# Reordering the queues of a ConvFFN up stage: additions out of PSUM ahead of the gated product, and a new order of operand sums and norm in the first pair

## The reference, cut to what matters

```python
D_FF = 2816
def conv_ffn(hn, buf, w_up, conv_w, conv_b, w_down):
    T = hn.shape[1]
    up = hn @ w_up                                   # 1024 -> 2 x 2816
    full = jnp.concatenate([buf.astype(up.dtype), up], axis=1)
    conv = sum(full[:, j:j + T] * conv_w[j] for j in range(CONV_W)) + conv_b
    a, gt = jnp.split(conv, 2, axis=-1)
    return (a * jax.nn.silu(gt)) @ w_down, full[:, T:]
...
    f, conv_state = conv_ffn(rmsnorm(x, P['norm_ffn'][l]), s_conv, ...)
    x = x + f
y = rmsnorm(x, P['norm_final'])
```

## Time and profile before

| | us |
|---|---|
| median of 3 runs (lowest, highest) | 2222.54 (2219.32, 2223.23) |
| the profiled execution, its own time | 2222.29 |
| its span, first to last instruction | 2220.2 |
| TensorE busy in the span | 2147.5 (97%) |
| VectorE, ScalarE, GpSimd busy | 1240.8, 757.2, 557.8 |

### The profile page before, as it was taken

The page is one execution under the profiler, slowest core; times in us unless marked ns, Lnnn a source line. Parts: engine busy times, 40 slices in busy tenths (PEclk is TensorE's granted clock), DMA queues, the critical chain, the costliest instruction groups (busy, mean ns, idle before and its releaser), DMA issues.

```text
span 2220.2 us, 35643 instructions
## 1 busy us (share of the span) xinstructions
PE 2147.5 (97%) x15110; PEld 2091.2 (94%) x15110; DVE 1240.8 (56%) x1526; ACT 757.2 (34%) x1094; POOL 557.8 (25%) x604
## 2 busy tenths in 40 slices
PE   7999999999999999999999999989999999999997
PEld 6999999999999999999999988989999999999997
DVE  6514755444456264246643234488888888854446
ACT  6313344233322322233321144254444444421113
POOL 6689910000000000000000000055555555410001
PEclk9999999999999999999999999999999999999999
DMA  7322114122422223244312152221222212343212
GB/s 277 115 77 66 66 57 172 60 77 89 153 98 77 69 87 115 77 162 174 123 47 86 48 225 116 87 69 63 81 71 71 79 64 81 111 174 124 86 66 77
DMA packets 66260, 222.79 MB, mean 100 GB/s; under 512 B 7584, under 2 KB 13024, under 8 KB 62416
## 3 DMA queue, kind: packets, MB, share of 16 engines
q1 hardware_dynamic: 46144, 129.70, 17.5%
q0 software_dynamic: 14816, 62.51, 7.5%
q10 hardware_dynamic: 5184, 28.98, 3.3%
HBM read 168.38 MB, written 51.78 MB: 99 GB/s over the span
## 4 chain that ended last, share of the span: by engine, by line
PE 77%; DVE 15%; issue 3%; ACT 2%; POOL 2%; DMA 1%; DVEq 0%; ACTq 0%; POOLq 0%
PE ps L305 19%; PE ps L308 19%; PE ps L306 19%; DVE WQ L3175 3%; PE ps L2785 2%; DVE CA L3224 2%; DVE CA L3223 2%; PE ps L2789 2%; PE ps L2786 2%; POOL UBA L2709 1%; PE ps L1981 1%; PE ps L2337 1%; PE ps L2313 1%; DVE UBA L3216 1%; DVE WL L299 1%
## 5 line engine op out<-in xcount | busy, mean ns | idle before, releaser
L305 PE MATMUL ps<-XH,WH 128*128 128x352 f32 (+1 forms) x1752 | 566.8, 325 | 5.6 <-ACT STAGE L365 3.1
L306 PE MATMUL ps<-XL,WH 128*128 128x352 f32 (+1 forms) x1560 | 491.9, 320 | 0.0
L308 PE MATMUL ps<-XH,WL 128*128 128x352 f32 (+1 forms) x1752 | 371.1, 320 | 0.0
L305 PEld LDWEIGHTS ps<-XH,WH 128*128 128x128 f32 x1752 | 330.2, 188 | 14.3 <-issue 10.2
L299 DVE TENSOR_TENSOR WL<-WRAW,WH 128x1024 fp32r<-128x1024 f32 x133 | 166.5, 1252 | 271.6 <-ACT WH L294 270.1
L306 PEld LDWEIGHTS ps<-XL,WH 128*128 128x128 f32 x1560 | 294.5, 189 | 0.1
L308 PEld LDWEIGHTS ps<-XH,WL 128*128 128x128 f32 x1752 | 292.4, 188 | 0.0
L294 ACT ACTIVATE WH<-WRAW 128x1024 fp32r<-128x1024 f32 x133 | 140.8, 1058 | 329.9 <-PE ps L308 311.7
L2785 PE MATMUL ps<-B,WQ 128*128 128x258 f32 x528 | 140.3, 287 | 19.3 <-DVE UBG L3216 18.9
L305 PE MATMUL ps<-HX,WH 128*128 128x352 f32 (+1 forms) x480 | 153.9, 322 | 3.0 <-DVE HX L3237 3.0
L306 PE MATMUL ps<-HX,WH 128*128 128x352 f32 (+1 forms) x480 | 151.9, 322 | 0.0
(11 more groups left out here) (622 smaller groups left out, 4868.6 us busy)
## 6 DMA issues: line engine op xcount, KB each, us to landing
WRAW<-in_wslabs SPq DMA_DIRECT2D x133, 512.0 KB, 3.6
WRAW<-in_wup SPq DMA_DIRECT2D x88, 256.0 KB, 2.7
scratch_spill<-STAGE SPq DMA_DIRECT2D x40, 516.0 KB, 2.7
ZS<-scratch_spill POOLq DMA_DIRECT2D x24, 516.0 KB, 5.3
scratch_h<-HOUT ACTq DMA_DIRECT2D x22, 516.0 KB, 2.7
HRAW<-scratch_h POOLq DMA_DIRECT2D x22, 516.0 KB, 5.8
XIN<-in_xT SPq DMA_DIRECT2D x8, 516.0 KB, 4.5
XR<-in_xT ACTq DMA_DIRECT2D x2, 2064.0 KB, 7.9
```

Source lines behind the costliest of these rows:

```text
L305: pe.matmul(out[t], WH[:, slot, w, :], xh(k, t), start=(k == 0), stop=False)
L306: pe.matmul(out[t], WH[:, slot, w, :], xl(k, t), start=False, stop=False)
L308: last = pe.matmul(out[t], WL[:, slot, w, :], xh(k, t), start=False, stop=(k == nk - 1))
```

## The change

Four things are done.

1. In VectorE's queue `product(f-1)` moves from ahead of d2 to behind b. In ScalarE's queue `store(f-1)`, which waits for it, moves behind the copies of P7 and the high parts of P7 and P2; the high part of P4 moves ahead of `now`.
2. Pair 0: the rests of B22 and of N3 2, 3 move from GpSimd to VectorE (table `E_PL` goes); the two last N4 differences move behind the norm; `norm_columns` stands ahead of P6 and the row of the norm is spread into banks 0 and 1 once b has read P2; P2 of pair 1, not P4 of pair 0, waits for the row. The weight operands of pair 1 are split in the order P1, P5, P6, P3, P7, P2, and GpSimd's sums of pair 1 no longer stand behind the scaling.
3. The loads of the convolution weights FW and FB move from GpSimd's queue to SyncE's.
4. Last pair: two of the four reloaded rows are raised and their rests made ahead of `product(20)` and `store(20)`, two behind.

```diff
 # sums: GpSimd
+        def pool_late_sums(pool, f):
+
             nc.gpsimd.tensor_tensor(A21, A21, A11, ALU.subtract).then_inc(s_sum.sem, 1)
...
-            for k in range(4):
-                rest("B22", k, y_of(k))
-            for k in range(2, 4):
-                rest("N3", k, XR[:, k, HALF:N])
+            pool_sums(pool, 1)
             pool.wait_ge(norm_rb, 2)
             pool_scale(pool, 0, 0)
-            pool.wait_ge(e_lo, E_LO["N4", 3])
-            pool.wait_ge(e_pl.sem, e_pl.at(6))
-            pool.dma_start(FW[:], I["ffn_w"]).then_inc(ffn_in.sem, 16)
-            pool.dma_start(FB[:], I["ffn_buf"]).then_inc(ffn_in.sem, 16)
-            pool_sums(pool, 1)
+            pool_late_sums(pool, 1)
...
 # TensorE, pair 0
+            norm_columns()
             pe.wait_ge(s_lo, W_AT["P6", 0])
             pe.wait_ge(u_ac, 1)
-            product("P6", slot_of("P6", 0), lambda k: pe.wait_ge(e_lo, E_LO["T2", k]))
-            norm_columns()
+            product("P6", slot_of("P6", 0), lambda k: pe.wait_ge(e_lo, E_AT["T2", k]))
...
+            pe.wait_ge(u_dv, DV_AT["b", 0])
             norm_spread()
...
 # ScalarE, pair f
             for f in range(1, NF):
-                if f == 1:
-                    act_product_hi(act, "P6", 1)
-                    act_product_hi(act, "P3", 1)
+                act_product_hi(act, "P4", f)
                 now(f - 1, 0)
                 if f > 1:
                     act.wait_ge(u_cv.sem, u_cv.at(2 * f - 2))
-                act_product_hi(act, "P4", f)
                 act_take(act, "P1", f, first_half(UB[f % 2][0]))
...
-                store(f - 1)
                 act_take(act, "P7", f, first_half(UB[f % 2][1]))
                 if f < NF - 1:
                     act_product_hi(act, "P7", f + 1)
                     act_product_hi(act, "P2", f + 1)
                 else:
+                    for kk in range(2):
+                        raise_h(0, kk)
                     slab_hi(1)
-            for kk in range(4):
+                store(f - 1)
+            for kk in range(2, 4):
                 raise_h(0, kk)
...
 # VectorE, pair f
-                product(f - 1)
-                if f == NF - 1:
-                    slab_lo(0)
                 join("d2", f)
                 if f < NF - 1:
                     dve_product_lo(dve, "P3", f + 1)
+                else:
+                    slab_lo(0)
                 join("a3", f)
                 if f < NF - 1:
                     dve_product_lo(dve, "P7", f + 1)
+                join("b", f)
+                if f == NF - 1:
+                    for kk in range(2):
+                        rest_h(0, kk)
+                product(f - 1)
+                if f < NF - 1:
+                    dve_product_lo(dve, "P2", f + 1)
                 else:
                     dve.wait_ge(u_pe, U_AT["P7", f])
                     slab_lo(1)
-                join("b", f)
-                if f < NF - 1:
-                    dve_product_lo(dve, "P2", f + 1)
                 join("c", f)
```

More of the change, by code:

```diff
@@ L2582, in program @@
         EARLY = [(x, m) for m in range(4) for x in ("B11", "T1")] + [("B21", k) for k in range(3)]
-        E_HI = {x: n + 1 for n, x in enumerate(
+        E_AT = {x: n + 1 for n, x in enumerate(
             EARLY + [("T2", 0), ("T2", 1), ("T2", 2), ("B21", 3), ("T2", 3)] +
             [(x, k) for x in ("B22", "N3", "N4") for k in range(4)])}
-        E_LO = {x: n + 1 for n, x in enumerate(
-            EARLY + [("B21", 3)] + [("T2", k) for k in range(4)] + [("N3", 0), ("N3", 1)] + [("N4", k) for k in range(4)])}
-        E_PL = {x: n + 1 for n, x in enumerate([("B22", k) for k in range(4)] + [("N3", 2), ("N3", 3)])}
+        C_AT = {x: n + 1 for n, x in enumerate(
+            [(x, k) for k in range(2) for x in ("N3", "T2", "N4")] +
+            [("N3", 2), ("T2", 2), ("N3", 3), ("T2", 3), ("N4", 2), ("N4", 3)])}
         u_pe, u_ac, u_dv = sem("u_pe"), sem("u_ac"), sem("u_dv")
@@ L2775, in pe_ffn, with product @@
         def pe_ffn(pe):
-            def product(p, w, k_wait=None, after=None):
+            def product(p, w, k_wait=None):
                 x = OPS[OP_OF[p]]
@@ L2802, in norm_spread @@
                 for c in range(2):
-                    last = pe.matmul(ps[:, 6 + c, :], ONES, SS[:, 512 * c:512 * c + 512], start=True, stop=True)
+                    last = pe.matmul(ps[:, c, :], ONES, SS[:, 512 * c:512 * c + 512], start=True, stop=True)
                 last.then_inc(norm_pe, 1)
@@ L2807, in norm_samples @@
                 pe.wait_ge(norm_act, 2 * 3 + 2)
[L2808 removed]
+                pe.matmul(ps[:, 0, 0:B], ONES, SS[:, T:N], start=True, stop=True).then_inc(norm_tail, 1)
             pe.wait_ge(s_lo, W_AT["P1", 0])
[L2811 removed]
+            pe.wait_ge(e_lo, E_AT["B11", 3])
             evacuated(pe, G_CO + 7)
@@ L3034, in act_ffn @@
             act_take(act, "P1", 0, first_half(UB[0][0]))
-            act.wait_ge(e_c.sem, e_c.at(3 * 3 + 2))
-            act_raise(act, "T2", 3, XR[:, 3, 0:HALF])
             act_product_hi(act, "P3", 0)
             act_product_hi(act, "P7", 0)
+            act.wait_ge(e_c.sem, e_c.at(C_AT["T2", 3]))
+            act_raise(act, "T2", 3, XR[:, 3, 0:HALF])
+            for k in range(4):
+                act.wait_ge(e_y.sem, e_y.at(k + 1))
+                act_raise(act, "B22", k, y_of(k))
             act.wait_ge(xr_out.sem, xr_out.at(16 * KT))
@@ L3041, in act_ffn @@
             act_take(act, "P5", 0, second_half(UB[0][1]))
-            for k in range(4):
-                act.wait_ge(e_y.sem, e_y.at(k + 1))
-                act_raise(act, "B22", k, y_of(k))
-            for k in range(4):
-                act.wait_ge(e_c.sem, e_c.at(3 * k + 1))
-                act_raise(act, "N3", k, XR[:, k, HALF:N])
-            act_product_hi(act, "P1", 1)
-            act_take(act, "P6", 0, second_half(UB[0][0]))
             act.wait_ge(norm_pe, 2 * 3 + 1)
@@ L3244, in dve_ffn @@
             dve_add_residual(dve, last)
+            for k in range(3):
+                dve.wait_ge(e_c.sem, e_c.at(C_AT["T2", k]))
+                dve_rest_of(dve, "T2", k, XR[:, k, 0:HALF])
             dve_gained_rest(dve, "B21", 3, XR[:, last, 0:HALF], GAIN[:, 3, last:KT])
-            for k in range(3):
-                dve_rest_of(dve, "T2", k, XR[:, k, 0:HALF])
             dve_n3_t2(dve, 3)
+            dve_sum(dve, KT * 3 + last, False, last % 2, N, 9 * 3 + last)
+            dve.wait_ge(e_c.sem, e_c.at(C_AT["T2", 3]))
             dve_rest_of(dve, "T2", 3, XR[:, 3, 0:HALF])
-            dve_sum(dve, KT * 3 + last, False, last % 2, N, 9 * 3 + last)
             dve_product_lo(dve, "P3", 0)
-            dve_product_lo(dve, "P7", 0)
-            dve.wait_ge(norm_dve, 9 * 3 + KT)
-            dve_n4(dve, 3)
+            for k in range(4):
+                dve_rest_of(dve, "B22", k, y_of(k))
             join("b", 0)
-            for k in range(2):
-                dve_rest_of(dve, "N3", k, XR[:, k, HALF:N])
-            dve_product_lo(dve, "P1", 1)
             dve.wait_ge(norm_act, 2 * 3 + 1)
```

103 lines of the change are left out of this document (58 added, 45 removed).

## The result

Measured side by side on one chip, 12 runs each, the changed kernel took 2225.02 us (median; 2223.48 to 2228.18), the kernel before 2221.78 (2219.32 to 2224.13). The ratio is 1.0018, with a 95% interval of 1.0009 to 1.0026: 3.2 us slower, a loss of less than 0.2%, but one whose interval lies wholly above 1. Forecast were 2227.4 with 2209 to 2235.

What follows compares the result with a forecast made beforehand. The prediction took VectorE's chain to set the steady pair's 21.7 us, TensorE needing at most 20.8. Its terms, +10.5 (steady pairs), -7.2 (pair 0 and 1) and +1.6 (last pair), summed to +4.9: 2227.4 us, range 2209 to 2235.

Steps and rivals of the forecast that it cites:

- The shared side: Steady pairs: VectorE's product and GpSimd's scaling exclude one another on shared SBUF access; join c starts 4.25 us after b.
- rival A: Steady pairs run at TensorE's pace, a3 coming early: -0.9 us a pair, about 2199 us in all; chance 20%.
- The sums between the taps: Steady pairs: GpSimd's WX, WY and WRAW, 1.2 us each, fall between the taps of UBA; those of UBG run free.
- Rival B: Steady pairs: sums stay out from between UBA's taps; +0.3 us a pair, evening out at 2222.6 us; chance 25%.
- The walk to the next b: VectorE's instructions in a steady pair, counted from b: next b at 22.1 us instead of 21.66, +0.45 in this parity.
- The term of the steady pairs: All 19 steady periods together: +0.55 us a pair, +10.5 us, with bounds of -17 to +19.
- Pair 0 and 1: Start of the up stage: shorter first wait, no 3.68 us norm wait; -7.2 us, with bounds of -12 to -3.
- The last pair: Last pair: the product delays the steps behind it by its length and one port turn; +1.6 us, between -2 and +4.
- nothing won: Last pair: the two rows raised early were counted as bringing no gain against the delay, within the +1.6 us.
- Rival C: Steady pairs: new 1 us waits at P1 and P3 lower the clock in some pairs; +5 to +8 more, 2234 us; chance 10%.
- TensorE's pace: Steady pairs: TensorE itself needs at most 20.8 us a pair, against the 21.7 set by VectorE's chain.

Runs made afterwards that it cites:

- e5: The changed kernel with join c ahead of the rest of P2 in VectorE's queue, the product staying behind b: 2216.4 us, 0.9973 of the kernel before.
- e4: The changed kernel with the product between d2 and the rest of P3, the store right behind the copy of P7: 2196.66 us, 0.9882 of the kernel before.
- e1: The changed kernel with the steady pairs' order (product, store, high part of P4) as before the change: 2215.6 us, 0.9973 of the kernel before.
- e2: The changed kernel with product and store placed as before, ScalarE's high part of P4 staying ahead of `now`: 2209.51 us, 0.9942 of the kernel before.
- e8: The changed kernel with one N4 difference of pair 0 ahead of the last residual addition again, as before: 2227.08 us in one run.
- e6: The changed kernel with the last pair as before, its four reloaded rows raised together behind c: 2226.31 us, 1.0022 of the kernel before.

## Why the prediction was right, step by step

- **The shared side.** Forecast: the product takes the turn, the scaling waits for it (near 3.0), the rest of P2 waits for the scaling (2.5), c comes at 4.25. Measured 2.94, 2.51, 4.17. This excluded rival A, which needed c within 2.5, and e5 shows the mechanism: a join in the same place does not wait.
- **The sums between the taps.** Forecast: GpSimd's WX, WY and WRAW fall between the taps of UBA and leave those of UBG free. The first tap took 3.44 instead of 1.28 (3.03 in the other parity, which is the one of the walk: near 3), the taps of UBG 1.28. Rival B needed the opposite.
- **The walk to the next b.** It was made for the parity with the shorter scaling of UBG, which in the changed kernel is the pair from b at 1680.00 on: rest of P5 17.07 after b (forecast 17.15), d2 18.27 (18.35), rest of P3 20.20 (20.3), next b 22.01 (22.1). The pair shown above is the other parity: 17.41, 18.62, 20.55, and 22.36 where the forecast had 22.6. Ahead of b the forecast counted five short steps in the pair before; d2, rest of P3, a3 and rest of P7 are four, and nothing else rests on it. What the product leaves behind, a wait for ScalarE's high part of 1.25, is the hole; e4 proves it by filling it.
- **The term of the steady pairs** was 10.5 (0.55 a pair) and measured 9.4 (0.49). From b to b the mean went from 21.52 to 22.07 in the parity of the walk and from 21.94 to 22.37 in the other: +0.55 (forecast 0.45) and +0.43 (forecast 0.6). So the two halves erred in opposite directions. The walk was right to 0.1, but was measured against the one pair of 21.66, longer than the mean, and the longer scaling of UBG added 0.30 to the period where it had added 0.42 before, not more.
- **Pair 0 and 1**: -7.2 forecast, -8.0 measured. P1 of pair 1 came at 26.74 (26.5), P6 at 35.54 (35.3), the 3.68 wait is gone; the new wait at P1 of pair 1 was 0.91 and not about 2, so TensorE was through with pair 0 some 1.3 us later than counted. P1 of pair 2 was to come at 52.9, which is what e1 and e2 have; the 1.0 less is the moved product in pair 1, which the walk had left out by saying that pair 1 runs as any. That the first wait at 1.12 leaves the clock at full was the reading of the earlier trace rows, and e8 confirms it, with the forecast's price of 1.5 us for a slow stretch.
- **The last pair**: +1.6 forecast, +2.6 measured, for reasons only half right. The product's length counts (1.1 up to the third block), but "nothing won" hid a loss and a gain of the split rows that cancel (e6), and the clock decides the last 1.5 from one profile to the next.
- **Rival C** failed: the new waits of the steady pairs are 0.45 to 0.90 us, and the clock was at 1.00 from 1500 to 1900 us.

The sum was +4.9, the measured parts +3.9 from the stage's start, the medians +3.2. Two terms were too high, by 1.1 and 0.8, and the third too low by 1.0; that the sum came within 1 us of the parts is partly luck. The forecast took 4.4 us as what tells this kernel from no change, and +3.2 lies under that; its likeliest case, 2223 to 2231, holds the result.

The forecast's own weak place was its alternatives. It saw the gap that the product had covered and priced it (2.2 paid, 1.15 gained), and yet treated a period of 20.8, its "TensorE's pace", as reachable only if GpSimd and VectorE did not exclude one another. e4 reaches 20.77 with the same exclusion. And 20.8 was no floor: it was "at most" what TensorE needs, and e4's rows put it at some 20.4.

**Open**: what decides whether a wait of 2.1 us lowers the clock (it did in the kernel before, not in e6), and how often the changed kernel's last pair takes 298.5 or 300.0. Not tried: the store moved alone, the loads of FW and FB back in GpSimd's queue, the rests of B22 back on GpSimd, and so how the -7.0 of pair 0 (e1, 52.97 less 60.00) divides among its parts.

## What to carry to other kernels

An instruction that stands in front of an urgent one is not simply in the way: if the one behind the urgent one has to wait for other engines, it covers that wait. Look for this hole before moving it, and move it into the hole, not past it. When a two-input SBUF instruction of VectorE must stand near a GpSimd one, count what is queued behind both, and put the instructions that read PSUM first. Moving one or two instructions within their queues was worth from +0.4 to -1.4 us a pair against the changed kernel, with the same instructions throughout.

## What the runs showed of the hardware

- Two waits of nearly one length at the same place, 2.16 and 2.11 us, left TensorE at 0.50 in one kernel and at 1.00 in another. In e1, waits of 0.58, 1.17 and 1.29 left it at full, and 2.83 was followed by 0.55 over three microseconds.
- A slow stretch has a price by its place: 1.1 to 1.5 us where TensorE is busy to the end behind it, next to nothing where it would have waited for another engine anyway.
- A small instruction pays for the whole turn of its neighbour: a tap on 8 elements took 0.23 us alone and 1.21 when a GpSimd sum of 512 elements came first.
